# Loads of the expert tables begun by two engines in place of one, in a two-layer encoder with product-key experts

## The reference

```
s = einsum(q, sub_keys); vals, idx = top_k(s, 16)        # 8 heads, 2 halves of 128 keys
experts, gates = top 16 of the 16 x 16 sums, softmax      # 128 experts of 16384 per token
ue = u_table[experts]; act = gelu(einsum('td,ted->te', h, ue))
ve = v_table[experts]; out = einsum('te,ted->td', gates * act, ve)
```

## Time and profile before

| | us |
|---|---|
| median of 3 runs (lowest, highest) | 1583.55 (1582.47, 1584.18) |
| the profiled execution, its own time | 1587.31 |
| its span | 1585.5 |
| TensorE busy | 1551.8 (98%) |
| VectorE busy | 1091.9 (69%) |
| GpSimd busy | 462.4 (29%) |
| ScalarE busy | 295.6 (19%) |
| moved by DMA | 531.83 MB, 335 GB/s in the mean |
| stage of the tables, layer 0 and 1 | 193 to 794 and 983 to 1579 in the span |

### The profile page before, as it was taken

One profiled execution on the slowest core, in us unless ns is written; L12 is line 12 of the kernel. 1 busy time (PEld: TensorE's weight loads), 2 busy tenths in 40 slices (PEclk: granted clock), 3 DMA queues, 4 the chain that ended last, 5 costly groups with the idle time before them and its releaser, 6 DMA issues.

```text
span 1585.5 us, 30461 instructions
## 1 busy us (share of the span) xinstructions
PE 1551.8 (98%) x11510; PEld 1454.8 (92%) x11510; DVE 1091.9 (69%) x2333; ACT 295.6 (19%) x632; POOL 462.4 (29%) x477
## 2 busy tenths in 40 slices
PE   8999999999999999999999999999999999999998
PEld 6778899999999999899977688999999999998998
DVE  5578899678846874544388778996788478644443
ACT  6385410100000000000066753001000000000000
POOL 0002044333433343333100020443333324433330
PEclk9999999999999999999999999999999999999999
DMA  6455599999999999999854264999999999999996
GB/s 245 162 147 190 178 351 358 385 402 408 409 409 409 371 400 409 409 410 410 340 182 151 80 200 172 348 367 388 399 408 409 409 408 403 406 409 409 409 410 248
DMA packets 150925, 531.83 MB, mean 335 GB/s; under 512 B 18736, under 2 KB 22080, under 8 KB 150464
## 3 DMA queue, kind: packets, MB, share of 16 engines
q1 hardware_dynamic: 88416, 321.43, 52.9%
q0 software_dynamic: 57056, 204.60, 33.2%
q10 hardware_dynamic: 5376, 4.81, 1.2%
HBM read 527.41 MB, written 1.06 MB: 333 GB/s over the span
## 4 chain that ended last, share of the span: by engine, by line
PE 86%; DMA 7%; DVE 4%; issue 2%; ACT 1%; ACTq 0%; POOL 0%; DVEq 0%; SPq 0%; POOLq 0%
PE ps L1940 34%; PE ps L1882 29%; PE ps L1694 4%; DMA raw<-stream 3%; PE ps L1709 3%; PE ps L1711 3%; PE ps L1710 3%; DMA big<-u_rows,own 2%; PE ps L1692 2%; PE ps L1893 2%; DMA big<-stream 1%; PE ps L1859 1%; PE ps L1829 1%; DVE big L1349 1%; PE ps L1691 1%
## 5 line engine op out<-in xcount | busy, mean ns | idle before, releaser
L1447 DVE SCALAR_TENSOR_TENSOR big<-big,own_act 128x1024 f32<-128x1024 f32 x192 | 246.5, 1284 | 208.1 <-PE ps L1940 111.2
L1349 DVE SCALAR_TENSOR_TENSOR big<-big 128x1024 f32<-128x1024 f32 x192 | 232.9, 1227 | 125.8 <-DMA big<-u_rows,own 94.3
L582 POOL DMA_INDIRECT big<-u_rows,own x192 | 209.2, 1089 | 338.3 <-DVE big L1349 320.5
L582 POOL DMA_INDIRECT big<-v_rows,own x192 | 201.4, 1049 | 342.0 <-DVE big L1447 321.0
L1940 PE MATMUL ps<-big 128*128 (+1 forms) x2048 | 294.9, 302 | 4.9 <-issue 0.2
L1940 PE MATMUL ps<-big,raw 128*128 (+1 forms) x2048 | 292.3, 301 | 3.7
L1940 PEld LDWEIGHTS ps<-big 128*128 128x128 f32 x2048 | 280.5, 190 | 16.6 <-issue 15.6
L1940 PEld LDWEIGHTS ps<-big,raw 128*128 128x128 f32 x2048 | 280.2, 190 | 12.1 <-issue 11.1
L1882 PE MATMUL ps<-big 128*128 128x160 f32 x2048 | 285.8, 300 | 0.4 <-DMA big<-stream 0.2
L1882 PE MATMUL ps<-big,raw 128*128 128x160 f32 x2048 | 285.1, 300 | 0.5 <-DMA raw<-stream 0.4
L1882 PEld LDWEIGHTS ps<-big 128*128 128x128 f32 x2048 | 279.9, 190 | 1.3 <-DMA big<-stream 0.9
(11 more groups left out here) (254 smaller groups left out, 1286.4 us busy)
## 6 DMA issues: line engine op xcount, KB each, us to landing
raw<-stream SPq DMA_DIRECT2D x353, 512.0 KB, 4.1
big<-stream SPq DMA_DIRECT2D x256, 512.0 KB
big<-u_rows,own POOLq DMA_INDIRECT x192
big<-v_rows,own POOLq DMA_INDIRECT x192
big<-keys ACTq DMA_DIRECT2D x2, 1024.0 KB, 7.8
big<-row_copy ACTq DMA_DIRECT2D x6, 256.0 KB, 5.5
x<-x_in SPq DMA_DIRECT2D x1, 1024.0 KB, 5.6
big<-big POOLq DMA_DIRECT2D x4, 256.0 KB, 3.4
```

The lines of the kernel that those rows point to most:

```text
L582: pool.indirect_dma_start(out=fetched[:, b, :], out_offset=None, in_=table, in_offset=bass.IndirectOffsetOnAxis(ap=own[:, 0, k:k + 1].bitc ...
L1349: dve.scalar_tensor_tensor(out=row, in0=row, scalar=1.0, in1=own_h[token_class(k)], op0=ALU.mult, op1=ALU.mult, accum_out=own_act[:, k:k + ...
L1447: dve.scalar_tensor_tensor(out=out_, in0=row, scalar=own_act[:, k:k + 1], in1=out_, op0=ALU.mult, op1=ALU.add).then_inc(row_used, 1)
```

## The change

The sync engine's loop of a layer begins only the even units. The odd ones are begun by ScalarE, in two places: in the u half behind each Gelu of a pair of units, and in the v half in a new loop over the pairs 64 to 123, which waits for `used` and begins one unit. ScalarE's Gelu of the dots, which stood right behind its last Gelu of a pair, moves into that loop, behind the odd unit of the pair 72 (`OWN_GELU_AT` = 128 + 16 = 144): it now also waits for `used` >= first + 146. Buffers, semaphores and the order of the work on the other engines are as they were.

```diff
+        OWN_GELU_AT = U_E + 16
...
                 with sp.Fori(0, 2 * U_E // DEEP - 1) as turn:
-                    for n in range(DEEP):
+                    for n in range(0, DEEP, 2):
                         sp.wait_ge(used, DEEP * turn + (first + n + 1))
                         sp.dma_start(deep(n), unit_at(turn, DEEP, first + DEEP + n)).then_inc(deep_landed[n], 16)
...
+                def odd_unit(pair):
+
+                    n = 2 * pair + 1
+                    act.dma_start(deep(n), stream[first + DEEP + n]).then_inc(deep_landed[n % DEEP], 16)
+
...
                     act.activation(G[:, 2 * pair:2 * pair + 2, :], ps[:, b:b + 2, 0:N], ACT.Gelu).then_inc(gelu_ready, 1)
-
-                act.wait_ge(row_used, 2 * FETCHES * l + FETCHES)
-                act.activation(own_act[:], own_act[:], ACT.Gelu).then_inc(own_gelu, 1)
+                    odd_unit(pair)
+
+                for pair in range(PAIRS, 2 * PAIRS - DEEP // 2):
+                    act.wait_ge(used, first + 2 * pair + 2)
+                    odd_unit(pair)
+                    if 2 * pair == OWN_GELU_AT:
+                        act.wait_ge(row_used, 2 * FETCHES * l + FETCHES)
+                        act.activation(own_act[:], own_act[:], ACT.Gelu).then_inc(own_gelu, 1)
```

## The result

The change costs 67 us: 1651.07 us (1650.3 to 1651.69, 4 runs) against 1583.87 us before (1582.47 to 1585.21, 4 runs), a ratio of 1.0417, 95% interval 1.0404 to 1.0429. The profiled execution took 1651.4 us, its span is 1649.6, 64.1 longer than before. The forecast was +36 us with a range up to 1645: the right way, about half of the size.

The account below looks back on a forecast made before the run. DMA bounds the kernel late in each layer, TensorE elsewhere. Costs 2 x (7 + 17 + 8.6) = 65.2 us less a gain of 29.3 give +35.9: 1619.5 us on the median of 1583.55, range 1600 to 1645.

Parts of the forecast that it names:

- What bounds the kernel: Late in each layer the DMA, full at 409 GB/s, with TensorE waiting for units; everywhere else TensorE, 2.174 us a unit.
- The share: Late in v, with three queues, the stream gets the 59% it needs; fetches get 0.70 a unit, where 0.86 are due.
- the first rival: DMA shares stay 1:1 between stream and fetches, leaving only the moved Gelu's cost: +17.2 us, 1600.8 us; chance 0.18.
- The gain: TensorE's waits for units late in both layers and at the end of layer 0's u table vanish: 29.3 us together.
- The wait at the start of v: After unit 133 TensorE waits for one-hots because VectorE's fetches are late: 7 us a layer, bounds 0 to 10.
- The late Gelu: Gelu of the dots makes VectorE 12.1 us late; TensorE waits 8.6 us a layer after unit 145.
- The end: At L1973, the fold product ending v, ten fetches are left: TensorE waits 17 us a layer, between 13 and 21.
- the low end: Wait for the last fetches in v at 1.28 us each, the bare transfer: 13 us a layer.
- The high end of the range: 1645 us: waits of 10 at v's start and 25 at its end, with fetch latency grown under three queues, +58 us.
- Shares stay: Stream and fetches keep 1:1 DMA shares; only the moved Gelu costs, 2 x 8.6 = +17.2 us, 1600.8 us; chance 0.18.
- Faster, since the fetches catch up: Late fetches use DMA time lost before; no wait at v's start, 2 us at its end: -8, 1575.5 us; chance 0.08.

Follow-up runs that it names:

- the late Gelu alone: Kernel before, all units begun by the sync engine, ScalarE's Gelu of the dots made to wait for used >= first + 146: 1605.97 us, ratio 1.0131.
- the split from 176 on: Against the kernel before: odd units from 177 on begun by ScalarE, all earlier ones by the sync engine, Gelu of the dots unmoved: 1606.22 us, ratio 1.0130.
- The eight buffers: Changed kernel with the Gelu of the dots behind pair 68's odd unit, plus 8 fetch buffers in place of 4 from fetch 112 on: 1619.71 us, ratio 1.0239.
- the Gelu back at pair 68: Changed kernel with the Gelu of the dots behind the odd unit of pair 68 (used >= first + 138) in place of pair 72: 1629.80 us, ratio 1.0280.

## Why the prediction was half right

**What bounds the kernel** held. Late in v the two layers were short of DMA, not of TensorE, and the moved bytes per second did not change (409 before, 410 after).

**The share** held to the number: 59 and 41% of the DMA, forecast so, in the queues of 700 to 760 us. So the round of queues seen with two at a time in the earlier trace rows goes on with three, as the Trainium skill says in DMA: Bandwidth & Descriptors, section Queues, rings and completion order. Its section Issuing engines are not separate DMA queues, by which a second engine saves issue time alone, does not hold where the DMA engines are full: here the stream's share rose from 51 to 59%, and the first rival falls with it. The rate of 0.70 fetches a unit gave 85 dots at unit 128 and 176 fetches at unit 248, as forecast in both places. That three queues which all had enough to move would get a third each is not shown: the two of the stream asked for less.

**The gain** was forecast at 29.3 us. The waits between units 168 and 248 gave 27.9, forecast 26.7. The other 2.6 us, at the end of layer 0's u table, were no gain of the change. The shortage in the earlier trace rows belongs to the execution that was profiled: units 104 to 128 took 55.5 us in it, 52.2 in the changed kernel, but 52.2 and 52.3 also with the late Gelu alone and with the split from 176 on, where the sync engine begins every unit up to there. With the late Gelu alone, where L1883 is `up`:

```profile
461.18 8.86 PE L1883 MATMUL ps<-big 128*128 128x160 f32 x64
469.87 8.86 PE L1883 MATMUL ps<-big,raw 128*128 128x160 f32 x64
```

**The wait at the start of v**: 7.8 and 7.5 us, forecast 7.

**The late Gelu**: VectorE waited 12.5 us, forecast 12.1; TensorE 8.3 us, forecast 8.6.

**The end** is one of the two steps that failed. Ten fetches were forecast to be left; it was eleven in layer 0 and ten in layer 1. The wait was 23.0 and 19.8 us, forecast 17: what was wrong is the price of one fetch. I had 1.28 us (the transfer) and 2.1 us (the way round four buffers) and took a value between. In layer 0 eleven adds came in 23.0 us, 2.1 each, in layer 1 ten in 19.8, 2.0 each. Layer 0's:

```profile
L1458 DVE SCALAR_TENSOR_TENSOR big<-big,own_act 128x1024 f32<-128x1024 f32 x11 | 14.2, 1287 | 9.9 <-DMA big<-v_rows,own 9.3
```

The row nearest to it, the first fetch with little beside it, had given just this. That is 8.8 us of the missing 31. The eight buffers showed what the low end would have needed: a wider ring, and in layer 0 a DMA without the next stage's four units, which the forecast had overlooked when it said that the stream was over.

**What was not in the sum at all, and is the larger step that failed: TensorE's clock.** Every wait of the forecast was priced as idle time. But TensorE's granted clock fell to half (1.2 GHz) in each wait, and it was still there for the first of what came after (0.81 and 0.79 in the mean of the four units after the first two waits, 0.57 over the fold product). This is 11.01 - 8.94 = 2.1 us over the four units after the first wait of layer 0, 11.19 - 8.94 = 2.2 after the second, 6.41 - 3.43 = 3.0 over the fold product, 7.3 us together. Layer 1 has 1.8, 2.1 and 2.7, so both have 13.9. The Trainium skill has it, in TensorE: Matmul & The Clock Gate, section What's actually happening: an array that has idled comes back at the lower clock. The trace of the kernel before had one small case, which I passed over, since the clock was 0.999 over the whole span. Between the two stages TensorE waited 2.16 us for VectorE; the granted clock was 0.51 from 896.4 to 899.8 us, and 16 products took 3.20 us where the next 16 took 1.95:

```profile
895.74 3.20 PE L2050 MATMUL ps<-big 128*128 128x128 f32 x16 [2.16 <-DVE big L1551]
...
900.55 1.95 PE L2050 MATMUL ps<-big 128*128 128x128 f32 x16
```

That, and the three longer waits which the forecast put in a layer, were reason enough to price it.

**The sum again.** 8.8 us of longer waits at the end and 13.9 us of clock make 22.7 of the 31.3 us that were missing. A further 2.3 us lie in units 64 to 88, most of them in layer 1, where VectorE was late for the first weights, a wait of which the forecast had no word. 1.7 us lie outside the two stages, 1.4 are gain that was forecast and didn't come, and the waits on one-hots were 0.7 us longer in all. What is left is 2.5 us. Each of the four waits on one-hots cuts a group of products for the weights in two, which costs it a little under 1 us more. (The medians give +67.2, the profiled executions +64.1; the difference is the 3.0 us under the gain.) The high end of the range, 1645, lays its +58 us on the profiled execution; on the median, from which the forecast was told, it would have been 1642. The measured time lies above either.

**The rivals.** Shares stay: fallen, by the queues. Faster, since the fetches catch up: fallen; the holes in the slices that it counted on were made larger by the change, 296 and 299 GB/s for 371 and 400. Fetches stop while VectorE waits for the Gelu (237 GB/s from 525 to 538.4 us), and the stream stops while TensorE waits for VectorE (185 from 538.4 to 548). With the Gelu back at pair 68 a part of the holes stays, 341 and 367. None of the experiments was faster than the kernel before.

## What to carry to other kernels

A second engine that starts transfers is not only a second pair of hands: it is a second seat at the DMA, and where the DMA is full the traffic behind it gains exactly what the others lose. Ask who the others are and who waits for them; here it was VectorE, whose late one-hots and late adds stopped TensorE for longer than the stream had. And price a new wait of TensorE with the slow stretch after it, not with the wait alone.

When an action moves into a loop that is paced by another counter, look for what in the whole program waits for it: a Gelu of 0.28 us that came six units after VectorE asked for it cost 21 us, because VectorE, which also serves TensorE, stood before it.

## What the runs showed of the hardware

Three queues shared the 16 DMA engines so that the two that needed less than two thirds together got all they asked for (59%), and the total stayed at 409 to 410 GB/s with two or three at work. A wait of TensorE of 3.78 us was followed by a product at half clock (6.53 us), one of 0.61 us was not (3.67 us). A gather of 128 rows of 4 KB through a ring of four buffers came once in 2.0 to 2.1 us while the DMA moved 251 to 263 of its 410 GB/s; with eight buffers, and nothing else on the DMA, VectorE's adds of such gathers followed each other in 1.4 us.
